# A hybrid GLA and RWKV-7 layer on one core: the first phase's input turned by transposing DMA transfers

## What is computed

```python
h = rms_norm(x, norm_pre)
p = jnp.einsum('btd,dc->btc', h, w_in).astype(f32)
# columns: GLA q, k, v, z_g, gd | RWKV shift columns | z_r
o_gla  = gla_recurrence(q, k, v, log_a, state)     # then norm per head, silu(z_g)
o_rwkv = rwkv7_recurrence(r, w, k, v, kk, a, state)  # then group norm, bonus, silu(z_r)
m = jnp.einsum('btc,cd->btd', concatenate([o_gla, o_rwkv], -1), w_out)
x = x + rms_norm(m, norm_post)
```

## Time and profile before

| | |
|---|---|
| runs, us | 2402.9, 2400.16, 2397.54 (median 2400.16) |
| profiled execution, us | 2393.93 |
| its span, first to last instruction | 2391.4 |
| mean granted TensorE clock | 0.993 |
| busy over the span: PE, ACT, DVE, POOL | 2298.5 (96%), 1451.7 (61%), 1242.9 (52%), 571.7 (24%) |

### The profile page before, as it was taken

How to read it: one execution, slowest core, us unless ns; L and a number is a source line. 1 busy time by engine, 2 the same in 40 slices (tenths; PEclk the granted TensorE clock), 3 DMA queues, 4 the chain that set the end, 5 groups by cost and what they waited for, 6 DMA issues and landing times. The chain is left out here.

```text
span 2391.4 us, 71777 instructions
## 1 busy us (share of the span) xinstructions
PE 2298.5 (96%) x31098; PEld 1726.9 (72%) x31098; DVE 1242.9 (52%) x2353; ACT 1451.7 (61%) x2837; POOL 571.7 (24%) x1069
## 2 busy tenths in 40 slices
PE   6999999999999998889999999999999998999998
PEld 5777777777777767777888888888888775544443
DVE  6333434333333333566777777777777776432222
ACT  7466666666666646456776667666777774543323
POOL 0000000000000001155554555455555555000000
PEclk9999999999999999999999999999999999999999
DMA  6112222222211111112222222222222234354443
GB/s 241 67 54 77 68 73 68 68 86 85 73 54 54 54 67 43 44 46 76 70 70 70 71 75 76 75 75 76 70 72 62 57 93 148 114 161 150 159 155 127
DMA packets 198777, 204.72 MB, mean 86 GB/s; under 512 B 108608, under 2 KB 151936, under 8 KB 194112
## 3 DMA queue, kind: packets, MB, share of 16 engines
q1 hardware_dynamic: 196304, 184.41, 26.0%
q10 hardware_dynamic: 2160, 15.73, 1.8%
HBM read 119.81 MB, written 80.28 MB: 84 GB/s over the span
## 5 line engine op out<-in xcount | busy, mean ns | idle before, releaser
L667 PE MATMUL d<-h,w_hi 128*128 128x256 f16 (+1 forms) x3264 | 526.1, 270 | 9.8 <-DVE w_lo L1107 8.1
L667 PE MATMUL d<-h,w_lo 128*128 128x256 f16 (+1 forms) x1632 | 436.6, 270 | 0.0
L1784 POOL TENSOR_TENSOR r_inv_tmp<-r_inv 64x30 f32<-64x30 f32 (+14 forms) x480 | 259.7, 541 | 450.9 <-DMA r_inv<-scratch_blocks 414.5
L667 PEld LDWEIGHTS d<-h,w_hi 128*128 128x128 f16 x3264 | 315.0, 98 | 60.7 <-issue 23.9
L1823 PE MATMUL r_d<-h,w_hi 128*128 128x256 f16 (+1 forms) x1824 | 299.8, 271 | 0.8 <-DVE carry_s L2361 0.8
L1786 POOL TENSOR_TENSOR r_inv<-r_inv,r_inv_tmp 64x30 f32<-64x30 f32 (+14 forms) x480 | 280.1, 584 | 37.6
L1823 PE MATMUL first<-h,w_hi 128*128 128x256 f16 x1664 | 283.7, 274 | 0.0
L1823 PE MATMUL r_d<-h,w_lo 128*128 128x256 f16 (+1 forms) x912 | 243.8, 270 | 0.0
L1823 PE MATMUL first<-h,w_lo 128*128 128x256 f16 x832 | 227.7, 274 | 0.0
L1727 POOL MEMSET r_run_s<- 128x128 f16 x1 | 0.2, 206 | 933.5 <-POOLq L357 933.5
L1823 PEld LDWEIGHTS r_d<-h,w_hi 128*128 128x128 f16 x1824 | 173.5, 99 | 37.5 <-issue 15.5
(11 more groups left out here) (314 smaller groups left out, 4720.2 us busy)
## 6 DMA issues: line engine op xcount, KB each, us to landing
h<-in_x SPq DMA_DIRECT2D x33, 512.0 KB, 4.0
r_ops<-in_x SPq DMA_DIRECT2D x33, 512.0 KB, 4.2
out_y<-r_ops SPq DMA_DIRECT2D x33, 512.0 KB, 2.9
scratch_hT<-h SPq DMA_DIRECT2D x16, 1024.0 KB, 7.0
h<-scratch_hT ACTq DMA_DIRECT2D x15, 1024.0 KB, 7.4
scratch_mg<-m_hl SPq DMA_DIRECT2D x33, 256.0 KB, 2.0
r_zr<-scratch_zr SPq DMA_DIRECT2D x33, 256.0 KB, 3.4
r_bon<-scratch_bonus SPq DMA_DIRECT2D x33, 256.0 KB, 4.6
```

Source lines behind the costliest of these rows:

```text
L667: mm = pe.matmul(out, lhs(k, a, w), rhs(k, a, w), start=(n == 0), stop=(n == len(terms) - 1))
L1784: step(pool.tensor_tensor(tmp, inv[0:n, 0:u, u:u + 1].to_broadcast([n, u, w]), inv[0:n, u:u + 1, u + 1:32].to_broadcast([n, u, w]), ALU.mult))
```

## The change

From tile 3 on (`DMA_FROM = 3`) `turn_x`, `high_h` and `low_h` are gone. `scaled_x` writes the scaled x as float16 into `junk` (which also takes the squares of stats), by token. A new step `rest_x` on DVE multiplies x by its scale once more, subtracts `junk` and writes the rest into a new tile `x_lo`. A new step `turn_dma` on SP issues 16 transposing transfers of 128x128 float16, eight from `junk` and eight from `x_lo`, straight into the two planes of `hT`. `stats` and `rest_x` of a tile wait until the transfers of the tile before have landed. For the first tile of a block turn_dma also waits until `hT` is free, that is until the last round of two blocks before has run and its store has landed. `q` and `put_h` wait for the transfers in place of `low_h`. In the list, stats of (b+1, 1) moves from behind gd to just ahead of att(1), the steps rest_x, turn_dma and get_x of two tiles later follow each stats, and put_h(b+1) moves behind stats of (b+2, 0). In setup one semaphore does the work of two.

```diff
@@ a_steps
     def stats(b, i):
         if b <= LAST:
-            steps.extend((j, tile_of(b, i)) for j in ("stats", "scaled_x"))
+            tile = tile_of(b, i)
+            steps.extend((j, tile) for j in ("stats", "scaled_x"))
+            if tile >= DMA_FROM:
+                steps.extend((j, tile) for j in ("rest_x", "turn_dma"))
+                if tile + 2 < NT:
+                    steps.append(("get_x", tile + 2))
...
     rnd("gd", "take_gd")
-    turn(0, 0)
-    stats(b + 1, 1)
     rnd("k", "take_k")
...
     rnd("up", "log_decay")
-    turn(0, 1)
     mean(0)
...
+    stats(b + 1, 1)
     att(1)
-    turn(1, 0)
     rnd("zr0", "tanh_z", "gate_z")
...
-    turn(1, 1)
-    if ahead:
-        steps.append(("put_h", b + 1))
     rnd("v0", "take_v")
     mean(1)
     rnd("v1", "take_v")
     if b + 2 <= LAST:
         stats(b + 2, 0)
+    if ahead:
+        steps.append(("put_h", b + 1))
...
@@ sync
+            def turn_dma(tile):
+                b, i = home_of(tile)
+                sp.wait_ge(h_low.sem, h_low.at(tile, 2))
+                if i == 0:
+                    sp.wait_ge(h_out.sem, h_out.at(b - 2, 1))
+                    sp.wait_ge(d_full.sem, d_full.at(A_NO[b - 2, a_rounds(b - 2)[-1]], 1))
+                for a, x in ((0, junk), (1, x_lo)):
+                    for k in range(KT):
+                        sp.dma_start(hT[:, b % 2, a, k, i * P:(i + 1) * P], x[:, k * P:(k + 1) * P],
+                                     transpose=True).then_inc(*h_turned.up(tile - DMA_FROM))
@@ tensor, round q
-                    pe.wait_ge(h_low.sem, h_low.at(last_tile(b), 2))
+                    if last_tile(b) < DMA_FROM:
+                        pe.wait_ge(h_low.sem, h_low.at(last_tile(b), 2))
+                    else:
+                        pe.wait_ge(h_turned.sem, h_turned.at(last_tile(b) - DMA_FROM, 16))
@@ scalar, stats
+                if tile > DMA_FROM:
+                    act.wait_ge(h_turned.sem, h_turned.at(tile - 1 - DMA_FROM, 16))
...
-                act.activation(x_tok[:, tile % 2, :], x_tok[:, tile % 2, :], ACT.Identity,
-                               scale=s[:, 2:3]).then_inc(*scaled_ok.up(tile))
+                to = x_tok[:, tile % 2, :] if tile < DMA_FROM else junk[:, :]
+                act.activation(to, x_tok[:, tile % 2, :], ACT.Identity, scale=s[:, 2:3]).then_inc(*scaled_ok.up(tile))
@@ vector
+            def rest_x(tile):
+                dve.wait_ge(scaled_ok.sem, scaled_ok.at(tile, 1))
+                if tile > DMA_FROM:
+                    dve.wait_ge(h_turned.sem, h_turned.at(tile - 1 - DMA_FROM, 16))
+                dve.scalar_tensor_tensor(out=x_lo[:, :], in0=x_tok[:, tile % 2, :], scalar=xs[:, tile % 2, 2:3],
+                                         in1=junk[:, :], op0=ALU.mult, op1=ALU.subtract).then_inc(*h_low.up(tile, 2))
```

More of the change, by code:

```diff
@@ L98, in setup @@
         loaded = ctx.enter_context(nc.semaphore("s_par_loaded"))
-        zeroed = ctx.enter_context(nc.semaphore("s_ident_zeroed"))
         made = ctx.enter_context(nc.semaphore("s_ident_made"))
@@ L109, in _ @@
         def _(pool):
-            pool.memset(ident[:, :], 0.0).then_inc(zeroed, 1)
-            pool.wait_ge(zeroed, 1)
+            pool.memset(ident[:, :], 0.0).then_inc(made, 1)
+            pool.wait_ge(made, 1)
             pool.affine_select(out=ident[:, :], in_=ident[:, :], compare_op=ALU.not_equal, fill=1.0,
@@ L116, in _ @@
                 pool.memset(consts[:, k:k + 1], v).then_inc(made, 1)
-            pool.wait_ge(made, 7)
+            pool.wait_ge(made, 8)
 CH = 64
@@ L174, in check @@
         assert self.seen == {i: self.n for i in range(self.size)}, (self.name, self.seen)
+DMA_FROM = 3
 SC = {"w0h": 0, "a0h": 4, "nkk": 8, "kah": 12, "ka1": 16, "rk": 20, "lnw": 24, "mu": 28, "mu1": 41}
@@ L250, in a_steps @@
         turn(1, 1)
-        steps += [("decayed", b), ("put_h", b + 1)]
+        steps.append(("decayed", b))
         stats(2, 0)
+        steps.append(("put_h", b + 1))
         return steps
@@ L385, in gla_phase @@
         junk = sb("junk", [P, D], F16)
+        x_lo = sb("x_lo", [P, D], F16)
         xs = sb("x_stats", [P, 2, 4])
@@ L459, in gla_phase @@
         scaled_ok = sig("x_scaled", 1, NT)
-        tr_full = sig("tr_full", 2, NT)
-        h_high = sig("h_high", 2, NT)
+        tr_full = sig("tr_full", 2, DMA_FROM)
+        h_high = sig("h_high", 2, DMA_FROM)
+        h_turned = sig("h_turned", 16, NT - DMA_FROM, 16)
         h_low = sig("h_low", 2, NT)
@@ L523, in get_x @@
                 if tile >= 2:
-                    sp.wait_ge(tr_full.sem, tr_full.at(tile - 2, 2))
+                    sp.wait_ge(h_low.sem, h_low.at(tile - 2, 2))
                     sp.wait_ge(scaled_ok.sem, scaled_ok.at(tile - 2, 1))
@@ L529, in put_h @@
                 n = tiles(b) * P
-                sp.wait_ge(h_low.sem, h_low.at(last_tile(b), 2))
+                if last_tile(b) < DMA_FROM:
+                    sp.wait_ge(h_low.sem, h_low.at(last_tile(b), 2))
+                else:
+                    sp.wait_ge(h_turned.sem, h_turned.at(last_tile(b) - DMA_FROM, 16))
                 sp.dma_start(t["hT"][b][:, :, :, 0:n], hT[:, b % 2, :, :, 0:n]).then_inc(*h_out.up(b))
@@ L535, in get_h @@
                 if b == 0:
-                    sp.wait_ge(tr_full.sem, tr_full.at(NT - 1, 2))
+                    sp.wait_ge(h_low.sem, h_low.at(NT - 1, 2))
                     sp.wait_ge(h_out.sem, h_out.at(0, 1))
@@ L571, in _ @@
             does = {"get_x": get_x, "put_h": put_h, "put_zr": put_zr, "put_mg": put_mg, "get_w2": get_w2,
-                    "get_h": get_h}
+                    "get_h": get_h, "turn_dma": turn_dma}
             def get_w1(n):
@@ L1117, in split_w2 @@
                    .then_inc(*w2_ok.up(0))
-            does = {"low_h": low_h, "take_k": take_k, "log_decay": log_decay,
+            does = {"low_h": low_h, "rest_x": rest_x, "take_k": take_k, "log_decay": log_decay,
                     "decayed": decayed, "gate_z": gate_z, "state_mid": state_mid, "mask": mask, "state": state,
```

## The result

The changed kernel takes 2651.95 us (median of four runs, 2648.39 to 2654.49) against 2401.53 for the kernel before in the same comparison: 1.104 times, 95% interval 1.1027 to 1.1056, some 250 us slower. 2598 was forecast and 2449 to 2860 given as the range. The sign was right, and so were two of the three places where TensorE waits. The price of a transfer was not, and with it fell the case that I took for the likeliest, in which the third place (q) has no wait.

A forecast was written before the change was run, and what follows sets the result against it. TensorE's own instructions were taken to bound the first phase. From 2393.9 us profiled, -26 (transposes) + 53 (out(1)) + 150 (weights) + 0 (q) + 21 (clock) = +198, plus 6 to the median: 2598 us, range 2449 to 2860.

The forecast's parts named there:

- the three places where TensorE waits: Outputs of the second tile, squares behind the second phase's weights, and q: 53, 150 and 0 us forecast.
- the case that I took for the likeliest: Transfer price s from 0.33 to 1.1 us, transfers hidden at q: 2490 to 2635 us, chance 0.50.
- The worth of the transposes: Tiles 3 to 32 on TensorE: 60 groups of four at 0.435 us, a gain of 26.1 us.
- The wait at out(1): Second tile's outputs wait for stats, scaled_x, rest_x and masks: 3.8 us in 14 blocks, 53 us.
- The price s of a transfer: SP or DMA time for each of turn_dma's 16 issues a tile: 1.0 us taken, between 0.32 and 3.2.
- the prediction's own signs: Profile signs: no wait at q, ordinary blocks near 56 us; if q waits for the transfers, the pace rules.
- The pace case: Rival with s above 1.1, one buffer pair, q waiting: about 2690 us at 1.31, 2856 at 1.67; chance 0.32.
- The weights: Weight pieces queue behind the transfers on SP, so squares waits in 8 blocks: 150 us taken.
- 2.8 + 16 s: Forecast wait in us at squares in each of 8 blocks with weights, s being one transfer's price.
- The transposed tile at q: Tile (b+1, 1), needed by q at the block's end: transfers hidden up to s = 1.1, 0 us.
- The clock: Granted clock may fall after each of 14 waits at out(1): 0 to 42 us, 21 taken.
- The rival of the other side: Faster: waits covered, TensorE alone binds, rest_x done by 360.0 at out(1): 2374 us; faster or the same, chance 0.05.

The follow-up runs named there:

- e4: Kernel before with the 240 float32 transposes of tiles 3 to 32 left out and nothing put in their place: 2371.86 us, 0.988 times.
- e7: Changed kernel with two transposing transfers a tile, weights fetched ahead of them, and stats of (b+1, 1) moved behind out(1): 2375.43 us, 0.990 times the kernel before.
- e1: Changed kernel with get_w2 ahead of stats of (b+2, 0), so the weights are issued before the 16 transposing transfers: 2481.27 us.
- e6: Changed kernel with two transposing transfers a tile and get_w2 ahead of stats of (b+2, 0): 2446.4 us, 1.019 times the kernel before.
- e3: Changed kernel with two transposing transfers a tile, each over all 1024 columns, in place of 16: 2485.2 us.
- e2: Changed kernel with 16 plain transfers of the same squares in place of the transposing ones, leaving h unturned: 2541.4 us.
- e8: Changed kernel, still 16 transposing transfers a tile, with buffers per tile, stats moved, SP's steps spread over the block, weights fetched ahead: 2380.63 us, 0.992 times the kernel before.

## Why the prediction held, and where it did not

- The worth of the transposes: 26.1 us forecast, 26.8 measured (e4). e7 has the same block of 52.23 us and takes 25.2 us less than the kernel before. Right, by the distance of starts.
- The wait at out(1): 3.8 us in each of 14 blocks forecast; 3.6 measured in 14 blocks where nothing else disturbs (e1, e6). Right in cause and size. In the changed kernel itself it sums to 34.4 and not to 53, for the reason given under e1.
- The price s of a transfer: 1.0 us taken, 1.3 measured. This is the step that failed. With no row for it, I took the middle of two rows a factor of ten apart, and put 0.50 on s from 0.33 to 1.1 and 0.32 on s above 1.1; the latter came. By the prediction's own signs the likeliest case is out: q waits, and a block without weights takes 58.8 us, not 56. The pace case's number at s = 1.31, about 2690 us, is 1.4% from the measured time, but only in part for its reason. Worked by its steps, the tile lands 58.0 us into a block without weights; yet in e3, where q never waits, such a block still takes 57.4 us. There it is out(1) and the clock that set the length, and the pace adds 0.3 to 1.4 us at q. (In its sum, stats at 30.8 us into the block is 30.5 by the rows, 358.1 - 327.64, which moves 2856 by some 2 us.) I had also given the lone issue's 0.32 us as the lower row for a stream; in a stream a plain issue costs 0.60 (e2).
- The weights: 150 us forecast at s = 1.0, 160.5 measured, 20.1 a block. With the 21.4 us measured for 16 s, 2.8 + 16 s says 24.2 us a block and 194 in all. The form was right (e1: without the order the wait is gone; e2 and e3: it follows 16 s). Its constant was some 4 us a block too high at this point: get_x, put_h and the two pieces were through 8.1 us after the first of them was issued, not 9.8, and TensorE itself came 2.6 us later to squares, since it had waited at q first. That 150 came so near 160.5 is luck in part: a price too low and a constant too high.
- The transposed tile at q: 0 forecast up to s = 1.1; at 1.3 it is 35.8 us, 2.3 to 2.9 us in each block with weights. 10.2 of these are one wait ahead of block 2. Block 1 has no att(1) and ends before tile 4 has landed. That I had not worked out, and it makes up, with the clock behind it, the 13 us ahead of block 2.
- The clock: 21 us taken between 0 and 42; some 44 measured by the windows (45.6 less 1.7), part of it behind squares and q. Of what is lost behind squares, the shorter wait at out(1) gives most back, as I had predicted. Where out(1) is the only wait, e6 gives the figure: 57.5 - 52.2 - 3.6 = 1.7 us a wait as a mean of 14, from nothing to 2.6.
- The sum: -27 + 34 + 160 + 36 + 44 = 247 of the 250 measured, in place of -26 + 53 + 150 + 0 + 21 = 198. The terms were off by -1, -19, +10, +36 and +23 in that order, and so cancel in part.
- The rival of the other side said that the waits are covered, and put the point at rest_x done by 360.0. e7 shows that this rival's 2374 us exists, 1 us off, but in another order of the list and with two transfers a tile.
- The Trainium skill's 1309 ns for a 128x128 DMA transpose ("VectorE: DVE Perf Modes", section "The three transpose paths") is near what a transposing issue costs SP here, 1.23 us, or 1.3 with the gaps. Whether that is the time it means, no run shows; from issue to landing it is 2.4 us. As a price of each 128x128 square it does not hold for SP: e3 turns eight of them for 1.245 us. The other end, a transposing transfer as fast as a plain one, is not borne out for 32 KB either: 1.23 us on SP against 0.60 (e2).

## What to carry to other kernels

An engine that is bound is relieved only if what replaces its work starts where the other engines wait for it: look for their idle time in the order of one block, and put the new steps there (e7), before asking what a transfer costs. With room, even sixteen transfers a tile gain 0.8% (e8). On an in-order queue, a burst of issues delays what stands behind it by its whole length; list who is queued behind, and fetch first what is needed next (e1). Fewer, larger transfers are the first thing to try when SP's own time is the length of the burst (e3).

## What the runs showed of the hardware

- A transposing transfer costs SP 1.23 us per instruction when it turns one 128x128 square of 16-bit elements, and 1.25 to 1.33 us when it turns eight; it lands in 2.4 us or 3.3 us. A plain transfer of 32 KB in the same stream costs 0.60 us and lands in 1.9 us (e2); alone, one of 256 KB costs 0.32.
- A wait of TensorE of 3.6 us was followed by 5.4 us at a granted clock of 0.50 in the changed kernel, by some 3.4 us in one block of e6 and by none in the block before it. Such a wait costs from nothing to 2.7 us more than its length, 1.7 in the mean of e6's 14.
- A float32 transpose of 128x128 takes TensorE 0.11 us in a stream of four (26.8 us for 240, e4), though its row reads 0.27.
